# Who issues the first row loads of the last part: ScalarE and the sync engine, or the sync engine alone

## The reference, cut to what matters

```python
# per token: 8 of 64 experts; each gives a row of 1024 numbers, scaled by its gate
routed = sum of the token's 8 expert rows
shared = (silu(h @ w_sh_gate) * (h @ w_sh_up)) @ w_sh_down
x = x + g2 * (routed + shared)
y = rms_norm(x, g_final)          # y_prompt (512 x 1024), y_sample (32 x 1024)
```

## Time and profile before

| | us |
|---|---|
| median of 3 runs (1299.84 to 1302.45) | 1300.3 |
| profiled execution, its own time | 1300.35 |
| its span in the profile | 1298.5 |
| last scatter issued by POOL | 1228.23 |
| first strip of the sample issued by SP | 1235.26 |
| first operation of DVE in the last part | 1242.08 |

### The profile page before, as it was taken

How to read it: one execution, slowest core, us unless ns; L and a number is a source line. 1 busy time by engine, 2 the same in 40 slices (tenths; PEclk the granted TensorE clock), 3 DMA queues, 4 the chain that set the end, 5 groups by cost and what they waited for, 6 DMA issues and landing times.

```text
span 1298.5 us, 19158 instructions
## 1 busy us (share of the span) xinstructions
PE 1180.6 (91%) x5813; PEld 497.2 (38%) x5813; DVE 429.0 (33%) x1098; ACT 214.7 (17%) x437; POOL 137.2 (11%) x155
## 2 busy tenths in 40 slices
PE   3899999998779998799999989999999999899964
PEld 1343444465424543243333333333333333333322
DVE  2113123155413448523233223232323233233257
ACT  2200100245400111111111111111111111111101
POOL 2000000000002010001111111111111111111100
PEclk9999999999789999899999999999999999899978
DMA  9965440297076000789979999899899679877396
GB/s 324 403 259 216 174 122 35 109 325 231 1 227 252 33 21 1 311 347 384 374 290 364 406 419 395 312 405 379 316 400 397 239 293 415 357 267 285 128 360 258
DMA packets 65772, 351.64 MB, mean 271 GB/s; under 512 B 11586, under 2 KB 11586, under 8 KB 32278
## 3 DMA queue, kind: packets, MB, share of 16 engines
q1 hardware_dynamic: 48766, 309.93, 62.0%
q0 software_dynamic: 15680, 37.05, 7.5%
q10 hardware_dynamic: 1240, 3.78, 0.8%
HBM read 336.03 MB, written 34.13 MB: 285 GB/s over the span
## 4 chain that ended last, share of the span: by engine, by line
PE 43%; DMA 10%; issue 7%; DVE 5%; SPq 3%; ACT 0%; POOL 0%; DVEq 0%; ACTq 0%; POOLq 0%
PE psum L1359 22%; PE psum L1385 9%; DMA sb_stream<-w_exp_up 9%; PE psum L1333 3%; PE psum L1806 2%; PE psum L1819 2%; PE psum L1373 1%; DMA sb_stream<-expert_rows 1%; PE psum L1365 1%; SPq L721 1%; PE psum L1349 1%; SPq L1284 1%; SPq L1408 1%; PE psum L1309 1%; DVE sb_work L2050 1%
## 5 line engine op out<-in xcount | busy, mean ns | idle before, releaser
L1359 PE MATMUL psum<-sb_stream,sb_convg 128*64 128x512 f32 x1664 | 377.9, 608 | 25.0 <-DMA sb_stream<-w_exp_up 22.7
L1359 PEld LDWEIGHTS psum<-sb_stream,sb_convg 128*64 128x64 f32 x1664 | 119.8, 140 | 239.6 <-issue 237.3
L1385 PE MATMUL psum<-sb_stream,sb_hbuf 128*64 128x512 f32 x832 | 190.0, 598 | 0.0
L1495 POOL DMA_INDIRECT expert_rows<-sb_attn,sb_row x52 | 52.2, 1004 | 544.4 <-DVE sb_token L1319 288.6
L1765 DVE TENSOR_TENSOR sb_hbuf<-psum,sb_hbuf 128x256 f32<-128x256 f32 x53 | 22.5, 424 | 233.8 <-ACT sb_hbuf L1552 233.8
L1385 PEld LDWEIGHTS psum<-sb_stream,sb_hbuf 128*64 128x64 f32 x832 | 55.1, 136 | 95.4 <-issue 89.2
L634 PE MATMUL psum<-sb_hT,sb_stream 128*128 128x512 f32 x192 | 86.4, 607 | 2.8 <-DMA sb_stream<-w_in 2.8
L1793 DVE TENSOR_SCALAR sb_attn<-psum,sb_now_gate 128x512 f32<-128x512 f32 x52 | 39.0, 751 | 149.0 <-PE psum L1385 149.0
L698 PE MATMUL psum<-sb_stream,sb_hT 128*128 128x512 f32 x192 | 86.2, 606 | 0.0
L1552 ACT ACTIVATE sb_hbuf<-psum 128x256 f32<-128x256 f32 x53 | 20.3, 383 | 390.6 <-PE psum L1359 389.3
L1333 PEld LDWEIGHTS psum<-sb_cst,sb_work 128*128 128x128 f32 x424 | 51.3, 194 | 43.0 <-issue 43.0
(11 more groups left out here) (310 smaller groups left out, 1025.6 us busy)
## 6 DMA issues: line engine op xcount, KB each, us to landing
sb_stream<-w_exp_gate SPq DMA_DIRECT2D x65, 1024.0 KB, 7.4
sb_stream<-w_exp_up SPq DMA_DIRECT2D x65, 1024.0 KB, 10.7
sb_stream<-w_exp_down SPq DMA_DIRECT2D x65, 1024.0 KB, 11.2
sb_stream<-w_ada SPq DMA_DIRECT2D x12, 2048.0 KB, 18.4
sb_stream<-expert_rows SPq DMA_DIRECT2D x7, 2048.0 KB, 20.2
sb_stream<-w_in SPq DMA_DIRECT2D x6, 2048.0 KB, 14.8
sb_stream<-cache_k SPq DMA_DIRECT2D x8, 1024.0 KB, 12.1
sb_stream<-cache_v SPq DMA_DIRECT2D x8, 1024.0 KB, 14.3
```

Source lines behind the costliest of these rows:

```text
L1359: last = pe.matmul(psum[lo:lo + LANE, 0, :].rearrange("p (a n) -> p a n", a=2), xT[:, k, lo:lo + LANE], gu[j][:, k, :, :], start=(k == 0), ...
L1385: last = pe.matmul(psum[lo:lo + LANE, 4 + n, :], hidT[:, k, lo:lo + LANE], dn[j][:, k, n * 512:(n + 1) * 512], start=(k == 0), stop=(k == 1))
L1495: pool.indirect_dma_start(expert_rows, bass.IndirectOffsetOnAxis(ap=row[:, u, :], axis=0), out[:, u, :], None, bounds_check=last_expert_ro ...
```

## The change

After stage 3's loop ACT waits for both `scat` semaphores as SP does and issues the loads of the first and the third prompt tile (four DMAs of 2 MB). SP keeps the four strips and the second tile (two DMAs of 2 MB). The fourth tile stays with SP in the last part. No load is added or dropped, and the semaphores that they count on and the places that they fill are the same.

```diff
                 for u in range(2):
                     sp.wait_ge(scat[u], 16 * nb)
                 load_sample(sp)
-                for j in range(1, 4):
-                    load_rows(sp, j)
+                load_rows(sp, 2)
...
                                 act.activation(out[:, u, 0:512], psum[:, 4, :], ACT.Copy, scale=now_gate[:, u:u + 1]).then_inc(s["out_lo"], 1)
+                for u in range(2):
+                    act.wait_ge(scat[u], 16 * nb)
+                load_rows(act, 1)
+                load_rows(act, 3)
```

## The result

| | before | after |
|---|---|---|
| median, us (5 runs each) | 1302.2 (1299.8 to 1302.7) | 1312.8 (1308.0 to 1314.5) |
| profiled execution, its own time / span | 1300.35 / 1298.5 | 1308.03 / 1305.9 |
| last scatter has landed, in the trace | 1231.96 | 1228.44 |
| T, the strips have landed, counted from that landing | 10.1 | 21.5 |
| from T to the end | 56.5 | 56.0 |

The ratio is 1.0083 (0.8% slower), with a 95% interval of 1.0063 to 1.0103. The direction was forecast. The size was not: 1308.7 was forecast, and 1312.8 lies at the edge of the range.

A forecast was written before the change was run, and what follows sets the result against it. The tail was taken as a DVE chain starting when the strips land. Late code 2.5, late start 2.5 and sharing 4.2, minus 0.7 for the first row wait, gave +8.5 us: 1308.7 us, range 1302 to 1313.

The forecast's parts named there:

- What bounds the kernel: Last part: a chain on DVE that begins when the strips land; prompt rows barely set it; span is T + 56.4.
- SP's four DMAs fewer: SP before the barrier: 1.9 us less issue time, all behind the strips, worth nothing as long as T is not under 1241.4.
- ACT's issue: After the scatters: ACT issues from 1232.1, the row stream starts 5 us sooner, gaining the 0.7 us of the first wait.
- Late start of a new queue: Strips on the DMA engines: their first packet comes later behind ACT's rows, 2.5 us lost (0 to 3.5).
- Late code: SP's last jump: its code comes by DMA behind ACT's rows, so the first strip is issued 2.5 us late (0 to 3.3).
- my own sign: SP's first strip issue in the timeline after: 1237 to 1238.5 expected; at 1235.3 the late code step is wrong.
- Sharing: Strips on the DMA engines: turns with ACT's row packets, 0.62 us each, cost 4.2 us (1.5 to 6.1).
- A: Rival: nothing moves, the strips get through nearly as before; T moves 0 to 3 us, 1300.5; chance 0.14.
- B: Rival: faster, the row stream limits the tail and all three row waits before L2043 go, 2.9 us; 1297.4; chance 0.04.
- C: Rival: mild, late start and sharing, but SP's code in time and no turns for completions; T +4 to +5, 1304; chance 0.19.
- D: Rival: worse, SP caught twice, at the jump and while issuing strips, sharing at its upper end; 1313 to 1316; chance 0.08.
- The row stream: Rows for tiles one to three: no new limit, all of them and the strips through by about 1266.

The follow-up runs named there:

- the repeat: The changed kernel run once more with no edit, nine runs; 1316.3 us against 1301.5 before, ratio 1.0098.
- the half tile's: Against the kernel before, ACT issues only the first half (2 MB) of the first tile, SP the strips and all the rest; 1301.6 us, ratio 1.0000.
- the fastest kernel: Against the kernel before: all five loads on ACT, sample in one DMA over 128 partitions, its add and fold ahead of the barrier; 1294.6 us, ratio 0.9938.

## Why the prediction was right in kind and short in size

*What bounds the kernel: held.* The tail is a chain on DVE that begins with T. From T to the end it takes 56.5 us before, 56.0 after, 54.9 in two other kernels; I had T + 56.4.

*SP's four DMAs fewer: worth nothing, held.* The barrier opened at 9.4 with SP's DMAs or without them, long before T.

*ACT's issue: held.* It came 0.1 us after the last scatter's landing. The first row wait went, as forecast.

*Late start of a new queue, 2.5 us: held.* The first packets of the strips come at 1233.4 to 1233.9, 3.4 us behind the issue at 1230.18, against some 0.8 on idle engines: 2.6. Here is that half microsecond by queue, and up to 1233.4 q10 alone had moved:

```profile
q10 hardware_dynamic: 7, 0.11, 58.6%
q1 hardware_dynamic: 3, 0.02, 11.7%
```

*Late code, 2.5 us: right in size where it came, but not in every execution.* SP's last jump took 1.95 to 1.97 us where it began ahead of ACT's rows or without them, 2.68 where it began 0.4 us behind their first issue (first tile on ACT), and 5.08, 4.66 and 5.23 where it began 1.0 to 1.5 us behind: 2.7 to 3.3 more. In the profiled execution of the kernel after it cost nothing: the first strip went out 1.7 us behind the landing, sooner than the 3.3 (1235.3 on the old scale) at which, by my own sign, the code step is wrong. There it was.

*Sharing, 4.2 us with 6.1 as the upper end: the step that failed.* From first packet to last landing the strips took 16.4 us (1233.6 to 1249.96) against 5.9 before: 10.5. The turns were counted right: 12 for each engine, at 1.32 us a pair, are 15.8 us (the 1.32 comes from the same stretch, so this agrees with the 16.4 but is no second proof). Their price was wrong. I took the row packets at 0.62 us, the value of a stretch in which rows ran alone, and let only the strips' own packets be slow. Measured, and without completions, the row packets took 1.06 us beside the narrow strips and 0.61 beside a wide one. The rate of the strips alone, 243 GB/s, stood in the earlier trace rows; I used it as an upper bound for their own packets and never for the other queue's. I also misreckoned there: 8 KB at 243 GB/s over 16 engines is 0.54 us, not 0.65, so that my upper end should have been 5.2 and not 6.1, still further from the 10.5. Why the narrow strips slow the other queue's packets stays open.

The terms by the first trace: first strip issued 1.6 us sooner, late start 2.6, sharing 10.5, together T + 11.5 (measured 11.4); from T on 0.5 less; tail +10.9. In the repeat T moved by 15.3, 3.2 for the later issue and 12.1 for issue to landing, and the tail by 13.8 (medians 14.9). With sharing at 10.5 my own sum would have been +14.8 with late code and about +12.3 without: 1315 and 1313.

*The rivals.* A (nothing moves) and B (faster) fall with T; B's mechanism was visible, since the row waits went, but worth half a microsecond to 1.5. C, with no late code, is what the profiled execution was in that term, and it lost more than C said. D's time, 1313 to 1316, is what the repeat reached, by another mechanism: one catch of SP, not two, and sharing far over its upper end. *The row stream* was not through at 34 from the landing (1266) as I had it, but at 41.5, for the same reason; that cost only one wait of 1.25 us.

*The Trainium skill.* "DMA: Bandwidth & Descriptors", section "Queues, rings and completion order", has each DMA engine serve its queues in turn, a packet at a time; 160 packets against 159 and 128 against 132 agree with it. The same page, section "Issuing engines are not separate DMA queues", says that DMAs started by several engines interleave on the same 16 DMA engines and that doing so saves only the time to issue them. The first half agrees with these counts. The second speaks of what is saved; the time that I derived from it, that nothing but issue time would move, was wrong: T moved by 11.4 us.

## What to carry to other kernels

A load that is wanted first belongs in the queue of the loads behind it and ahead of them; from a second queue it got every second turn here, and it, or the load beside it, came later. Before a transfer is put beside another, look at the rate that it has alone: here a narrow one at 243 GB/s alone took the pair down to 251. An engine that is free sooner is worth using for the whole ordered stream, not for a part of it, and the gain ends where the next release (here the barrier) stands.

## What the runs showed of the hardware that I had not expected

POOL's drain at the barrier took the same time in every kernel here. By line L1389 (durations ns, first and last start), kernel after, then before:

```profile
L1389 POOLq DRAIN  x1: 8807/8807/8807, 1228.9 to 1228.9; - x1
```

```profile
L1389 POOLq DRAIN  x1: 8807/8807/8807, 1232.4 to 1232.4; - x1
```

It was 8.807 us in all twelve traces, and the barrier opened 9.4 to 9.5 us behind the last scatter's landing in eleven of them (11.3 in the half tile's). The half tile's is the one in which SP's drain was later, behind its row issues that ended at 10.9. Until the barrier opens no engine enters the last part, so that in these kernels strips that land sooner than that gain nothing unless their work stands ahead of the barrier, as in the fastest kernel. That drain, not SP's, was the last release of the barrier; I had put it down to SP.
